# Parameter rows issued later, first gated products taken by token half, and three more convolution taps per tile moved into the mix turns

## The chip, the cores and the metric

The kernel runs on one core of one Trainium2 chip. The metric is the device time of one launch in microseconds (us). The core has TensorE (PE, matrix products; its weight loads are shown apart as PEld), VectorE (DVE), ScalarE (ACT), GpSimd (POOL) and SyncE (SP, which here only issues DMAs). Each engine works through its own queue in order and waits on semaphores that the others raise.

## What is computed

A block of a language model on 1024 tokens of width 1024, and behind it an attention block on the same tokens, in float32. Only the first part of the first block is touched:

```python
h = rmsnorm(x, g_mix[i])
z = jnp.einsum("bsd,dn->bsn", h, w_in[i])
a_val, a_gt = z[..., :o1], z[..., o1:o2]
sc_b, sc_c, sc_v = z[..., o2:o3], z[..., o3:o4], z[..., o4:o5]
gate_logits = z[..., o5:] + b_gate[i]
g_a = jax.nn.sigmoid(gate_logits[..., :D_MODEL])
g_b = jax.nn.sigmoid(gate_logits[..., D_MODEL:])
a = a_val * jax.nn.sigmoid(a_gt)
a = causal_dwconv(a, conv_a_w[i]) + conv_a_b[i]      # 31 taps, 512 channels
a = jax.nn.silu(layernorm(a, ln_a_g[i], ln_a_b[i]))
y_a = jnp.einsum("bsc,cd->bsd", a, w_a_out[i])
s = sc_b * causal_dwconv(sc_c * sc_v, conv_b_w[i])   # 3 taps
y_b = jnp.einsum("bsc,cd->bsd", s, w_b_out[i])
x = x + jnp.einsum("bsd,de->bse", g_a * y_a + g_b * y_b, w_o[i])
```

Behind it come a gated feed-forward part, a second gate, the attention block and the output; the change leaves them as they are, but for the count of a semaphore.

## The kernel before

All activations lie transposed: channels on the 128 partitions, the 1024 tokens along the row. Every matrix product is made of three products of split operands (high by high, low by high, high by low). A "slab" is 128 output channels of a weight: SP loads it into one of two `raw` buffers, POOL splits it into `whi` and `wlo` (L421, L422, L424), and PE takes it. A "job" is one such product, written to one of two pairs of PSUM banks (job number modulo 2): `gemm` (L482) waits until the pair is free and the slab is split, and issues for each of the 8 (or 4) blocks of input channels 6 matmuls of 512 tokens, so 48 (or 24) in all. DVE or ACT read the pair and raise `pair_free`. So PE can run at most about one pair of jobs ahead of DVE. POOL starts a slab's split when PE begins the slab before it.

The stages that the change touches, in order:

1. The x stage. Eight token tiles of x (128 tokens by 1024) are loaded by SP into two buffers `x_nat`; for each, ACT squares it and sums (L973), DVE scales the sum (L1286), ACT takes the root (L975), DVE the reciprocal (L1288) and the product `x_scaled` (L1292), PE transposes it in 8 blocks (L524), ACT copies it to `xa_hi` (L979) and DVE the remainder to `xa_lo` (L1296). Ahead of all this the queue of ACT issues the DMAs of the parameter rows (L953 to L967), 24 small loads into `rows`. Behind the eight tiles PE transposes the three blocks of `rows` (L552), DVE copies them to the table `tab` (L1299), ACT makes `silu_c` of it (L983), and only then PE begins the products.
2. The glu stage: four turns, each two jobs of 48 matmuls. ACT takes the sigmoid of the first (L988), DVE multiplies the second by it into `glu_pad` (L1342), and then does the first N1 = 14 of the 31 taps of the long convolution on that tile (`tap`, L1311 and L1315), each a scalar_tensor_tensor over 128x1024 that waits for the one before.
3. The short stage: four turns of three jobs. DVE does a 3-tap convolution (L1354 to L1362), N2 = 14 more taps of a tile of the long one, the product L1368, and the remainder `xb_lo` (L1373).
4. The mix stage: eight turns `mix_b`, then eight `mix_a`, each a gate job of 48 matmuls and a product job of 24. ACT takes the sigmoid of the gate (L1005), DVE the product (L1384 for mix_b). Behind the products of turns 0 and 1 DVE does the last N3 = 3 taps of two tiles each. Then it adds the four tiles (L1404, L1407) and takes the product of turn 2; PE sums over channels with a matrix of ones (L578) between turns 2 and 3; DVE subtracts the mean (L1411), ACT squares (L1012), PE takes column sums behind turn 3 (L531) and broadcasts the reciprocal root behind turn 4 (L541). ACT copies it to `rbc` (L1017), and in turn 5 DVE scales the four tiles (L1426), ACT makes the silu (L1022) and the high half (L1024), DVE the low half (L1430), tile by tile through one buffer. ACT takes the sigmoid of turn 5 only behind that. The first product job of mix_a needs the result.

Order on each queue is written out by hand; there is no planner.

Of the kernel before, what the change touches and what calls it, by code (L numbers as in the profile page):

```python
# [4 lines left out]
F32 = mybir.dt.float32  # L5
# [92 lines left out]
def build_program(nc, A, out, ydram):  # L98
# [41 lines left out]
    sqj = at("sq_junk", [P, D], F32, o_r + 5 * KB4)  # L140
# [105 lines left out]
    def settle(engine):  # L246


        engine.wait_ge(sem("consts_in"), 32)


    def sync_program(sp):
# [16 lines left out]
        sp.dma_start(xn[:, 0, :], A["x"][0, 0:P, :]).then_inc(sem("x_in0"), 16)  # L269
        sp.dma_start(gbc[:, :], A["g_mix"][0:1, :].to_broadcast([P, D])).then_inc(sem("g_in"), 16)  # L270
        sp.dma_start(xn[:, 1, :], A["x"][0, P:2 * P, :]).then_inc(sem("x_in1"), 16)
        slab8(L, w_in, DC, True)
        slab8(L + 1, w_in, 0, True)
        for t in range(2, 8):
            sp.wait_ge(sem("xs_ready"), t - 1)
            sp.dma_start(xn[:, t % 2, :], A["x"][0, t * P:(t + 1) * P, :]).then_inc(sem(f"x_in{t % 2}"), 16)
# [196 lines left out]
    def tensor_program(pe):  # L473
# [101 lines left out]
        mix_turns("mix_b", XBh[:, 4:8, :], XBl[:, 4:8, :], 1, 3)  # L575
# [4 lines left out]
        mix_turns("mix_b", XBh[:, 4:8, :], XBl[:, 4:8, :], 3, 4)  # L580
        column_sums(T[1], 8, 0, sem("ln_v"), 10)
        mix_turns("mix_b", XBh[:, 4:8, :], XBl[:, 4:8, :], 4, 5)
        broadcast(T[2][:, 0:1024].rearrange("p (t n) -> p t n", n=P), 8, 1)
        mix_turns("mix_b", XBh[:, 4:8, :], XBl[:, 4:8, :], 5, 8)
# [6 lines left out]
        for u in range(2):  # L591
            pe.wait_ge(sem(f"x_in{u}"), 8 * 16)
# [344 lines left out]
    def scalar_program(act):  # L937
# [8 lines left out]
        act.dma_start(rotm[:, :], A["rotate"]).then_inc(sem("consts_in"), 16)  # L946
        act.wait_ge(sem("consts_set"), 1)
# [22 lines left out]
        for t in range(9):  # L970
            if t < 8:
                act.wait_ge(sem(f"x_in{t % 2}"), 16 * (t // 2 + 1))
                fn(sqj[:, :], xn[:, t % 2, :], ACT.Square, accum_out=ssq[:, t:t + 1]).then_inc(sem("n1_sq"), 1)  # L973
                act.wait_ge(sem("row_var"), t + 1)
                fn(sd[:, t:t + 1], var[:, t:t + 1], ACT.Sqrt).then_inc(sem("row_sd"), 1)  # L975
            if t >= 1:
                J = Lin(JOBS["x"] + t - 1)
                act.wait_ge(job_done, J.val(1))
                fn(XAh[:, :, (t - 1) * P:t * P], pair(J).rearrange("p (m n) -> p m n", n=P), ACT.Copy).then_inc(sem("x_hi"), 1)  # L979

        act.wait_ge(sem("tab_ready"), 1)
        for k, name in enumerate(("c_2", "c_ctx_2")):
            fn(cs[:, :, k], tab[:, COL[name]:COL[name] + KD], ACT.Silu).then_inc(sem("cs"), 1)  # L983
        with act.Fori(0, KC) as i:
# [3 lines left out]
            fn(T[0][:, 0:S], pair(J), ACT.Sigmoid).then_inc(*one(free(J)))  # L988

# [17 lines left out]
        gate_sigmoid("mix_b", 0, 3, 8 + 5)  # L1007
        for i in range(4):
# [4 lines left out]
        gate_sigmoid("mix_b", 3, 4, 8 - 3)  # L1013
        root(8, 1)
        gate_sigmoid("mix_b", 4, 5, 8 - 3)
        act.wait_ge(sem("bc_pe"), 1)
        fn(rbc[:, :], PS[:, ST:ST + S], ACT.Copy).then_inc(sem("rbc_ready"), 1)  # L1017
        for i in range(4):
            act.wait_ge(sem("ln_n"), i + 1)
            if i >= 1:  # L1020
                act.wait_ge(sem("branch_lo"), 4 + i)
            fn(T[3][:, 0:S], T[1 + i % 2][:, 0:S], ACT.Silu, scale=col("ln_a_g", i), bias=col("ln_a_b", i)).then_inc(sem("a_silu"), 1)  # L1022
            act.wait_ge(sem("a_silu"), i + 1)
            fn(XBh[:, i, :], T[3][:, 0:S], ACT.Copy).then_inc(sem("branch_hi"), 1)  # L1024
        gate_sigmoid("mix_b", 5, 8, 8 - 3)
# [228 lines left out]
    def vector_program(dve):  # L1254
# [27 lines left out]
        dve.wait_ge(sem("g_in"), 16)  # L1282
        for t in range(9):
            if t < 8:
                dve.wait_ge(sem("n1_sq"), t + 1)
                ts(var[:, t:t + 1], ssq[:, t:t + 1], 1.0 / D, EPS, ALU.mult, ALU.add).then_inc(sem("row_var"), 1)  # L1286
                dve.wait_ge(sem("row_sd"), t + 1)
                nc.vector.reciprocal(rcp[:, t:t + 1], sd[:, t:t + 1]).then_inc(sem("row_rcp"), 1)  # L1288
# [3 lines left out]
                stt(xs[:, t % 2, :], xn[:, t % 2, :], rcp[:, t:t + 1], gbc[:, :], ALU.mult, ALU.mult).then_inc(sem("xs_ready"), 1)  # L1292
            if t >= 1:
                J = Lin(JOBS["x"] + t - 1)
                dve.wait_ge(sem("x_hi"), t)
                tt(XAl[:, :, (t - 1) * P:t * P], pair(J).rearrange("p (m n) -> p m n", n=P),  # L1296
                   f32(XAh[:, :, (t - 1) * P:t * P]), ALU.subtract).then_inc(*one(free(J)))
        dve.wait_ge(sem("tab_pe"), 1)
        nc.vector.tensor_copy(tab[:, :], PS[:, ST:ST + 3 * P]).then_inc(sem("tab_ready"), 1)  # L1299
# [578 lines left out]
```

## Time and profile before

| | us |
|---|---|
| median of three runs | 2226.7 |
| lowest and highest | 2226.05, 2227.9 |
| the profiled execution, as timed | 2228.41 |
| its span in the trace | 2226.6 |

| engine | busy us | share of span |
|---|---|---|
| PE | 2069.8 | 93% |
| PEld | 1711.0 | 77% |
| DVE | 1184.2 | 53% |
| ACT | 453.3 | 20% |
| POOL | 745.3 | 33% |

Times in the trace are counted from the start of the span. The page has a strip of each engine's busy share in 40 slices of 55.7 us; DVE stands at 4, 6, 8, 9, 9, 9, 5 in the first seven, and at 1 to 6 after. A busy PE is not a PE at its peak: its granted clock is a column of its own.

### The profile page before, as it was taken

To read this page: it belongs to the slowest core of one execution; us is meant where nothing else is said; L and a number is where in the kernel's file an instruction comes from. 1 tells how busy PE (TensorE), PEld (TensorE's weight loads), DVE (VectorE), ACT (ScalarE), POOL (GpSimd) and SP (SyncE) were. 2 spreads that over 40 slices of the span, in tenths; PEclk is the share of its full clock that TensorE was granted. 3 is DMA by queue.
4 is the path that set the end of the run, shared out by engine and by line. 5 is a ranking of instruction groups with operands and counts; after the bars stand their busy time and mean duration, and the time that the engine had idled before them with its cause. 6 is when DMAs were issued, how large, how long until landed. Compare 5 with 4: busy or idle time off the path is not lost.

```text
span 2226.6 us, 24771 instructions
## 1 busy us (share of the span) xinstructions
PE 2069.8 (93%) x9621; PEld 1711.0 (77%) x9621; DVE 1184.2 (53%) x1128; ACT 453.3 (20%) x558; POOL 745.3 (33%) x540
## 2 busy tenths in 40 slices
PE   4988999999998999999999999989689988999998
PEld 3876777788786788888888888768468867888877
DVE  4689995211543655655565655744441635556521
ACT  4100002200221100000000000233331125555511
POOL 1333454445332333333333333633132420212121
PEclk9999999999999999999999999999699998999999
DMA  4111111132113122112222112211131201000032
GB/s 127 47 38 38 43 39 42 42 92 74 57 38 114 48 66 67 47 52 71 75 66 66 47 47 75 76 29 38 29 112 31 90 15 25 10 11 1 1 123 85
DMA packets 176897, 122.04 MB, mean 55 GB/s; under 512 B 8820, under 2 KB 160321, under 8 KB 176833
## 3 DMA queue, kind: packets, MB, share of 16 engines
q1 hardware_dynamic: 175552, 118.77, 17.8%
q10 hardware_dynamic: 1280, 2.35, 0.3%
q8 instruction: 48, 0.79, 0.1%
q14 instruction: 17, 0.13, 0.0%
HBM read 112.71 MB, written 8.39 MB: 54 GB/s over the span
## 4 chain that ended last, share of the span: by engine, by line
PE 67%; DVE 17%; issue 4%; ACT 4%; POOL 4%; DMA 3%; DVEq 1%; ACTq 1%; SPq 0%; POOLq 0%
PE ps L482 55%; DVE conv_a L1315 8%; DMA raw<-in_w_up 2%; PE ps L764 2%; POOL wlo L424 1%; PE ps L531 1%; POOL rbc L443 1%; DVE prob L1694 1%; PE ps L541 1%; PE ps L797 1%; PE ps L799 1%; PE ps L778 1%; PE ps L798 1%; PE ps L775 1%; PE ps L781 1%
## 5 line engine op out<-in xcount | busy, mean ns | idle before, releaser
L424 POOL TENSOR_TENSOR wlo<-raw,whi 128x1024 fp32r<-128x1024 f32 (+2 forms) x162 | 455.4, 2811 | 13.5
L421 POOL TENSOR_TENSOR small<-ones 128x1 f32<-128x1 f32 x166 | 50.5, 304 | 1210.5 <-PE ps L482 1021.4
L482 PE MATMUL ps<-xb_hi,whi 128*128 128x512 f32 x1216 | 384.3, 398 | 42.4 <-DVE xb_lo L1593 16.4
L482 PE MATMUL ps<-xa_hi,whi 128*128 128x512 f32 x1184 | 374.9, 398 | 34.8 <-DVE t L1369 8.1
L482 PE MATMUL ps<-xb_lo,whi 128*128 128x512 f32 x1216 | 379.9, 394 | 0.0
L482 PE MATMUL ps<-xb_hi,wlo 128*128 128x512 f32 x1216 | 379.6, 394 | 0.0
L482 PE MATMUL ps<-xa_lo,whi 128*128 128x512 f32 x1184 | 368.7, 393 | 0.0
L482 PE MATMUL ps<-xa_hi,wlo 128*128 128x512 f32 x1184 | 368.3, 392 | 0.0
L482 PEld LDWEIGHTS ps<-xb_hi,whi 128*128 128x128 f32 x1216 | 228.9, 191 | 102.3 <-DVE xb_lo L1593 15.9
L482 PEld LDWEIGHTS ps<-xa_hi,whi 128*128 128x128 f32 x1184 | 223.7, 191 | 85.9 <-issue 34.2
L482 PEld LDWEIGHTS ps<-xb_lo,whi 128*128 128x128 f32 x1216 | 231.8, 191 | 49.5
L482 PEld LDWEIGHTS ps<-xb_hi,wlo 128*128 128x128 f32 x1216 | 231.6, 190 | 49.2
L482 PEld LDWEIGHTS ps<-xa_lo,whi 128*128 128x128 f32 x1184 | 225.4, 190 | 47.9
L482 PEld LDWEIGHTS ps<-xa_hi,wlo 128*128 128x128 f32 x1184 | 224.6, 190 | 47.6
L1315 DVE SCALAR_TENSOR_TENSOR conv_a<-glu_pad,tab,conv_a x120 | 199.5, 1662 | 20.7 <-DVE conv_a L1315 19.9
L422 POOL TENSOR_SCALAR whi<-raw 128x1024 fp32r<-128x1024 f32 (+2 forms) x162 | 174.1, 1075 | 0.2 <-issue 0.2
L1063 ACT ACTIVATE t<-t 128x1024 f32<-128x1024 f32 x22 | 23.3, 1061 | 515.2 <-DVE t L1486 515.2
L461 POOL TENSOR_SCALAR prob<-prob,small 128x1280 f32<-128x1280 f32 x32 | 43.0, 1343 | 229.5 <-DVE small L1703 229.5
L1499 DVE TENSOR_TENSOR resid<-ps,resid 128x1024 f32<-128x1024 f32 x80 | 97.8, 1222 | 35.0 <-PE ps L482 33.8
L1481 DVE TENSOR_TENSOR t<-ps,rbc 128x1024 f32<-128x1024 f32 x22 | 26.9, 1224 | 135.0 <-PE ps L482 130.2
L1486 DVE SCALAR_TENSOR_TENSOR t<-t,tab,t 128x1024 f32<-128x1024 f32 x44 | 93.4, 2122 | 6.2 <-DVE t L1483 1.4
L1686 DVE TENSOR_TENSOR pt_lo<-ps,pt_hi 128x512 fp32r<-128x512 f32 (+1 forms) x96 | 56.3, 598 | 40.7 <-ACT pt_hi L1179 40.6
(320 smaller groups left out, 2275.5 us busy)
## 6 DMA issues: line engine op xcount, KB each, us to landing
raw<-in_w_in SPq DMA_DIRECT2D x52, 512.0 KB, 3.8
raw<-in_w_up SPq DMA_DIRECT2D x44, 512.0 KB, 4.0
raw<-in_w_down SPq DMA_DIRECT2D x22, 512.0 KB, 3.6
w_mod<-in_w_mod SPq DMA_DIRECT2D x40, 256.0 KB, 2.8
x_nat<-in_x SPq DMA_DIRECT2D x8, 512.0 KB, 3.6
x_columns<-in_x SPq DMA_DIRECT2D x8, 512.0 KB, 5.1
raw<-in_w_o SPq DMA_DIRECT2D x8, 512.0 KB, 3.8
raw<-in_w_ple_gate SPq DMA_DIRECT2D x8, 512.0 KB, 3.8
```

The lines of the kernel that those rows point to most:

```text
L421: nc.gpsimd.tensor_tensor(small[:, 30 + slab.slot:31 + slab.slot], ones[:, 0:1], ones[:, 0:1], ALU.mult)
L422: nc.gpsimd.tensor_scalar(hi, src, 1.0, 0.0, ALU.mult, ALU.add).then_inc(sem("split_hi"), 1)
L424: nc.gpsimd.tensor_tensor(lo, src, f32(hi), ALU.subtract).then_inc(split_done, 1)
L461: nc.gpsimd.tensor_scalar(Pr[t % 2][:, :], Pr[t % 2][:, :], rsum4[:, t % 4:t % 4 + 1], 0.0, ALU.mult, ALU.add).then_inc(sem("p_scaled"), 1)
L482: ins = mm(dst[j], w, r[j], start=first and f, stop=last and l)
L764: last = nc.tensor.transpose(PS[:, o:o + P], Pr[a][:, k * P:(k + 1) * P], ident[:, :])
L1063: fn(T[2][:, 0:S], T[1][:, 0:S], ACT.Gelu_apprx_tanh).then_inc(sem("gelu"), 1)
L1315: stt(tile(conv, i), tile(gpad, i, k, k + S), dcol("conv_a_w", i + 4 * k), tile(conv, i), ALU.mult, ALU.add).then_inc(sem("conv_tap"), 1)
L1481: tt(T[0][:, 2:2 + S], pair(Jg), rbc[:, :], ALU.mult).then_inc(*one(free(Jg)))
L1486: stt(T[1][:, 0:S], T[0][:, w:w + S], dcol("conv_f_w", n + (k + NF * w)), T[1][:, 0:S], ALU.mult, ALU.add).then_inc(sem("fc_tap"), 1)
L1499: tt(R[:, m, :], pair(J + m), R[:, m, :], ALU.add).then_inc(*one(free(J + m)))
L1686: tt(PTl[:, k0:k1, cols], PS[:, o:o + (k1 - k0) * P].rearrange("p (t n) -> p t n", n=P), f32(PTh[:, k0:k1, cols]), ALU.subtract).then_inc( ...
```

## The change

What it does, part by part:

- SP: x is loaded into eight tiles of `x_nat` (now in the space of `xb_hi`); tiles 0 and 1 one by one, the first slab, tiles 2 and 3 in one DMA, tiles 4 and 5 (behind the first `x_scaled`), the second slab, tiles 6 and 7 (behind the second).
- ACT: a Sqrt on a constant stands ahead of the x stage. The parameter rows are issued behind the eight tiles. The square of tile t+2 and the root of tile t+1 stand ahead of the copy of tile t.
- The transposes of x write to the other half of PSUM. PE does the tiles 0 to 4, then the first glu job on tokens 0 to 511 in pieces between the transposes of tiles 5, 6 and 7, then the second job on these tokens, then both on tokens 512 to 1023; then the rows are transposed. `silu_c` no longer stands ahead of the products.
- N1 is 12, N2 13, N3 6. The last taps, 24 in all, are done 8 each behind the products of mix_b turns 0, 1 and 2; the adds come behind the product of turn 3.
- The sum with ones stands behind turn 4, the column sums behind turn 5, the broadcast behind turn 6, and the normalisation, silu and split in turn 7, in place in `conv_a`, with ACT no longer waiting for the low half of the tile before.

The core of the diff:

```diff
-    xn = at("x_nat", [P, 2, D], F32, o_r)
+    xn = at("x_nat", [P, 8, D], F32, o_xbh)
...
+        x_rows(0, 1, "x_in0")
+        sp.dma_start(gbc[:, :], A["g_mix"][0:1, :].to_broadcast([P, D])).then_inc(sem("consts_in"), 16)
+        x_rows(1, 1, "x_in1")
         slab8(L, w_in, DC, True)
+        x_rows(2, 2, "xn_in2")
+        sp.wait_ge(sem("xs_ready"), 1)
+        x_rows(4, 2, "x_in0")
         slab8(L + 1, w_in, 0, True)
...
+        pe.wait_ge(sem("consts_in"), 48)
+        for t in range(5):
+            x_transposes(t)
+        pe.wait_ge(split_done, 1)
+        pe.wait_ge(pair_free[0], 2)
+        pe.wait_ge(pair_free[1], 2)
+        glu_half(0, 0, range(0, 3))
+        x_transposes(5)
+        glu_half(0, 0, range(3, 7))
+        x_transposes(6)
+        glu_half(0, 0, range(7, 8))
+        pe.wait_ge(split_done, 2)
+        glu_half(1, 0, range(0, 3))
+        x_transposes(7)
+        glu_half(1, 0, range(3, 8))
+        pe.wait_ge(pair_free[0], 4)
+        pe.wait_ge(pair_free[1], 4)
+        glu_half(0, 1, range(KD))
+        glu_half(1, 1, range(KD))
         pe.wait_ge(sem("rows_in"), N_ROW_DMAS * 16)
...
-        pe.wait_ge(sem("cs"), 2)
-        pe.wait_ge(pair_free[0], 4)
-        pe.wait_ge(pair_free[1], 4)
-        with pe.Fori(0, KC) as i:
+        with pe.Fori(1, KC) as i:
...
-        mix_turns("mix_b", XBh[:, 4:8, :], XBl[:, 4:8, :], 1, 3)
+        mix_turns("mix_b", XBh[:, 4:8, :], XBl[:, 4:8, :], 1, 5)
         pe.wait_ge(sem("ln_v"), 3)
...
+        act.wait_ge(sem("consts_set"), 2)
+        fn(sd[:, 12:13], ones[:, 0:1], ACT.Sqrt)
...
+        x_square(0)
+        x_root(0)
+        x_square(1)
+        for t in range(8):
+            if t < 6:
+                x_square(t + 2)
+            if t < 7:
+                x_root(t + 1)
+            J = Lin(JOBS["x"] + t)
+            act.wait_ge(job_done, J.val(1))
+            fn(XAh[:, :, t * P:(t + 1) * P], x_pair(J).rearrange("p (m n) -> p m n", n=P), ACT.Copy).then_inc(sem("x_hi"), 1)
...
-        N1 = 14
+        N1 = 12
...
+        glu_product(0)
+        dve.wait_ge(sem("tab_pe"), 1)
+        nc.vector.tensor_copy(tab[:, :], PS[:, ST:ST + 3 * P]).then_inc(sem("tab_ready"), 1)
...
-        N3 = 3
+        N3 = 6
...
+        for m in range(3):
+            mix("mix_b", m, m + 1, False)
+            last_taps(8 * m, 8 * m + 8)
+        mix("mix_b", 3, 4, False)
...
-        for i in range(5):
+        for i in range(6):
             if i < 4:
-                if i >= 2:
-                    dve.wait_ge(sem("a_silu"), i - 1)
-                tt(T[1 + i % 2][:, 0:S], conv[:, i, :], rbc[:, :], ALU.mult).then_inc(sem("ln_n"), 1)
-            if i >= 1:
-                dve.wait_ge(sem("branch_hi"), 4 + i)
-                dve.wait_ge(sem("ln_n"), i)
-                tt(XBl[:, i - 1, :], T[3][:, 0:S], f32(XBh[:, i - 1, :]), ALU.subtract).then_inc(sem("branch_lo"), 1)
-        mix("mix_b", 5, 8, False)
+                tt(conv[:, i, :], conv[:, i, :], rbc[:, :], ALU.mult).then_inc(sem("ln_n"), 1)
+            if i >= 2:
+                dve.wait_ge(sem("branch_hi"), 3 + i)
+                tt(XBl[:, i - 2, :], conv[:, i - 2, :], f32(XBh[:, i - 2, :]), ALU.subtract).then_inc(sem("branch_lo"), 1)
+        mix("mix_b", 7, 8, False)
```

## Rows read from the trace of the kernel before

**Rows 1.** The page: the chain that ended last, by engine, then by line.
```profile
PE 67%; DVE 17%; issue 4%; ACT 4%; POOL 4%; DMA 3%; DVEq 1%; ACTq 1%; SPq 0%; POOLq 0%
```

**Rows 2.** Windows: stretch, length, busy (instructions) of PE, PEld, DVE, ACT, POOL, clock, DMA.
```profile
70.70:443.70 373.00, 343.67 (x1466) 278.96 (x1466) 282.78 (x184) 46.06 (x42) 152.74 (x102) 0.96 0.14 40
152.00:160.00 8.00, 5.93 (x14) 4.68 (x15) 7.23 (x5) 1.03 (x1) 4.41 (x3) 0.58 0.01 2
1573.00:1604.00 31.00, 17.45 (x46) 11.08 (x46) 12.23 (x21) 10.06 (x11) 2.10 (x3) 0.50 0.00 0
```

**Rows 3.** Waits of PE, 71 to 444 us: us in total, times, longest.
```profile
PE ps L482 <- DVE t L1369: 8.1, 3, 6.3
PE ps L482 <- DVE glu_pad L1342: 6.9, 2, 4.3
PE ps L482 <- ACT t L1005: 5.2, 1, 5.2
PE ps L578 <- DVE t L1407: 3.9, 1, 3.9
PE ps L482 <- DVE xb_lo L1373: 3.7, 1, 3.7
PE ps L482 <- DVE t L1354: 1.5, 1, 1.5
```

**Rows 4.** Timeline of the start: start us, us, engine, line; idle before.
```profile
11.39 0.33 ACTq L967 DMA_DIRECT2D rows<-in_c_ctx  x1
13.04 1.06 ACT L973 ACTIVATE sq_junk<-x_nat 128x1024 f32<-128x1024 f32 x1
17.69 1.94 PE L524 MATMUL ps<-ident,x_scaled 128*128 128x128 f32 x8 [17.69 <-DVE x_scaled L1292]
41.33 1.97 PE L524 MATMUL ps<-ident,x_scaled 128*128 128x128 f32 x8 [1.68 <-DVE x_scaled L1292]
46.75 1.21 PE L482 MATMUL ps<-xa_hi,whi 128*128 128x512 f32 x2 [2.81 <-ACT silu_c L983]
49.47 1.05 PE L482 MATMUL ps<-xa_hi,whi 128*128 128x512 f32 x2
51.48 0.62 PE L482 MATMUL ps<-xa_hi,whi 128*128 128x512 f32 x2
70.85 1.23 DVE L1342 TENSOR_TENSOR glu_pad<-ps,t 128x1024 f32 x1 [24.60 <-PE ps L482]
```

**Rows 5.** DMA issues in narrow windows of the start: count, KB each, median us to landing.
```profile
x_nat<-in_x SPq DMA_DIRECT2D x1, 512.0 KB, 4.1
raw<-in_w_in SPq DMA_DIRECT2D x2, 512.0 KB, 9.8
```

**Rows 6.** Groups of DVE, 71 to 347.3 us: busy us, mean ns, idle before.
```profile
L1315 DVE SCALAR_TENSOR_TENSOR conv_a<-glu_pad,tab,conv_a x120 | 199.5, 1662 | 20.7 <-DVE conv_a L1315 19.9 <-DVE conv_a L1311 0.7
```

**Rows 7.** Splits (L424) in the same stretch: length, POOL busy (count), clock, DMA.
```profile
71.00:347.30 276.30, 76.05 (x24) 0.97 0.14 42
```

**Rows 8.** Timeline of DVE around one split, four taps.
```profile
81.75 1.29 DVE L1315 SCALAR_TENSOR_TENSOR conv_a<-glu_pad,tab,conv_a  x1 [0.18 <-DVE conv_a L1315]
83.22 1.96 DVE L1315 SCALAR_TENSOR_TENSOR conv_a<-glu_pad,tab,conv_a  x1 [0.18 <-DVE conv_a L1315]
85.36 3.15 DVE L1315 SCALAR_TENSOR_TENSOR conv_a<-glu_pad,tab,conv_a  x1 [0.18 <-DVE conv_a L1315]
```

**Rows 9.** Timeline of the norm's steps, 347 to 408 us.
```profile
347.45 3.48 PE L578 MATMUL ps<-t,ones 128*128 128x512 f32 x4 [3.86 <-DVE t L1407]
385.47 1.88 PE L541 MATMUL ps<-t,ones 128*128 128x512 f32 x4
388.44 4.90 DVE L1426 TENSOR_TENSOR t<-conv_a,rbc 128x1024 f32<-128x1024 f32 x2 [1.56 <-ACT rbc L1017]
406.38 1.28 ACT L1005 ACT_TABLE_LOAD   x1
407.67 1.11 ACT L1005 ACTIVATE t<-ps,tab 128x1024 f32<-128x1024 f32 x1
```

More of the change, by code:

```diff
@@ L220, in pair, with x_pair @@
         return PS[0:p, 1024 * job.slot + a:1024 * job.slot + b]
+    def x_pair(job):
+        return PS[:, ST + 1024 * job.slot:ST + 1024 * (job.slot + 1)]
     def f32(ap):
@@ L542, in broadcast, with x_transposes, glu_half @@
             last.then_inc(sem("bc_pe"), 1)
-        pe.wait_ge(sem("consts_in"), 32)
-        for t in range(8):
+        def x_transposes(t):
             pe.wait_ge(sem("xs_ready"), t + 1)
-            transposes(Lin(JOBS["x"] + t), [xs[:, t % 2, k * P:(k + 1) * P] for k in range(KD)])
+            if t >= 2:
+                pe.wait_ge(pair_free[t % 2], t // 2)
+            for k in range(KD):
+                last = nc.tensor.transpose(x_pair(Lin(t))[:, k * P:(k + 1) * P], xs[:, t % 2, k * P:(k + 1) * P], ident[:, :])
+            last.then_inc(job_done, 1)
+        def glu_half(u, c, ks):
+            J, L = Lin(JOBS["glu"] + u), Lin(SLABS["glu"] + u)
+            q = slice(H * c, H * (c + 1))
+            for k in ks:
+                last = split_products([pair(J, H * c, H * (c + 1))], whi[:, L.slot, k * P:(k + 1) * P], wlo[:, L.slot, k * P:(k + 1) * P],
+                                      [XAh[:, k, q]], [XAl[:, k, q]], k == 0, k == KD - 1, 1 if c and k == 0 else None)
+            if c:
+                last.then_inc(job_done, 1)
+        pe.wait_ge(sem("consts_in"), 48)
[17 more added lines that the diff above has]
+        glu_half(1, 1, range(KD))
         pe.wait_ge(sem("rows_in"), N_ROW_DMAS * 16)
@@ L968, in scalar_program, with glu_sigmoid @@
                 r += n
[L970 to L984, printed above, removed]
+        def glu_sigmoid(i):
             J = Lin(JOBS["glu"], 2, i)
@@ L988, in scalar_program @@
             fn(T[0][:, 0:S], pair(J), ACT.Sigmoid).then_inc(*one(free(J)))
+        glu_sigmoid(0)
+        act.wait_ge(sem("tab_ready"), 1)
+        for k, name in enumerate(("c_2", "c_ctx_2")):
+            fn(cs[:, :, k], tab[:, COL[name]:COL[name] + KD], ACT.Silu).then_inc(sem("cs"), 1)
+        with act.Fori(1, KC) as i:
+            glu_sigmoid(i)
         act.wait_ge(*free(Lin(JOBS["short"] - 1)))
@@ L1335, in mod_mac, with glu_product @@
                 stt(acc, w, cs[:, k, n:n + 1], acc, ALU.mult, ALU.add).then_inc(sem("mod_mac"), 1)
-        N1 = 14
-        with dve.Fori(0, KC) as i:
+        N1 = 12
+        def glu_product(i):
             J = Lin(JOBS["glu"], 2, i)
@@ L1343, in vector_program @@
             dve.wait_ge(*free(J + 1))
+        glu_product(0)
+        dve.wait_ge(sem("tab_pe"), 1)
+        nc.vector.tensor_copy(tab[:, :], PS[:, ST:ST + 3 * P]).then_inc(sem("tab_ready"), 1)
+        dve.wait_ge(sem("tab_ready"), 1)
+        for k in range(N1):
+            tap(0, k, k)
+        with dve.Fori(1, KC) as i:
+            glu_product(i)
             for k in range(N1):
                 tap(i, k, i * N1 + k)
-        N3 = 3
+        N3 = 6
         N2 = TAPS_A - N1 - N3
@@ L1376, in vector_program, with last_taps, mix @@
                     tap(i, k, i * N2 + (KC * N1 + k - N1))
-        def mix(name, a, b, add, taps=False):
+        def last_taps(a, b):
+            for n in range(a, b):
+                i, k = n // N3, n % N3
+                tap(i, N1 + N2 + k, KC * (N1 + N2) + n)
+        def mix(name, a, b, add):
             with dve.Fori(a, b) as m:
@@ L1384, in mix @@
                     tt(tile(R, m + (5 if a < 3 else -3)), pair(J + 1), T[0][:, 0:S], ALU.mult).then_inc(*one(free(J + 1)))
-                    for v in range(2 if taps else 0):
-                        i = m * 2 + v
-                        for k in range(N1 + N2, TAPS_A):
-                            tap(i, k, i * N3 + (KC * (N1 + N2) + k - N1 - N2))
                 else:
```

77 lines of the change are left out of this document (43 added, 34 removed).

## The prediction

> **What bounds the kernel now.** I read the page first. PE is busy 93% of the span, yet the chain that ended last goes by DVE for 17% of it [rows 1]: there is a stage in which DVE sets the pace. The strip of the page puts it in the first seven slices. The windows then give its size. Call G the moment at which DVE can take the first gated product (70.85 us, the last of rows 4). PE's first product of mix_a begins at 443.7. Between 70.7 and 443.7 PE is busy 343.7 of 373.0 us [rows 2], and it waits 29.3 us in all, in every row for DVE or for something that stood behind DVE [rows 3]. The reader should see in these rows that no wait is for a DMA or a split.
>
> How much of that PE needs at full clock: 1440 matmuls (3 glu pairs of 96, 12 short jobs of 48, 8 mix turns of 72). Two take 0.62 us and overlap by a third [rows 4]; 48 of them run in 10.9 us, which is 0.227 each, so 326.9 us. The column sums 1.7, the broadcast 1.88 less overlap, 1.7, and the sum with ones, which ran at the low clock for 3.48, 1.75 at the high one [rows 9]: 332.1 in all. Busy less needed is 11.6 us: that is the clock. A stretch with a 4.3 us wait in it was granted 0.58 of the full 2.4 GHz [rows 2]. So between G and mix_a up to 40.9 us are to be had, 29.3 of waits and 11.6 of clock.
>
> Ahead of G lie 70.85 us. ACT issues parameter rows until 11.7 and squares its first tile at 13.04 [rows 4], though the tile was issued at 0.74 and landed 4.1 later [rows 5]. The transposes start at 17.69 and come 3.38 apart, (41.33 - 17.69)/7; the first product waits 5.4 us more, for the table and silu_c; the first matmuls run at the low clock (two in 1.05 instead of 0.62) [rows 4]. Behind 443.7 PE's order and its waits are as before, relative to one another, so what is gained up to there is kept.
>
> **Part 1, the start: G.** ACT begins tile 0 at 4.9. From the first square to the first transposes took 4.65 with a table load of 1.28 inside; that load is now done before, so the transposes of tile 0 start at 8.3. Tile 1 then waits: ACT has the square of tile 2 ahead of the root of tile 1, and tiles 2 and 3 come behind the first slab. The two slabs of before landed 9.8 us after their issue at 2.1 to 3.0, with five loads of 512 KB in flight [rows 5]; six are now ahead, less the rows' small packets. I take 13.5. Square, root, reciprocal and product (1.25, 0.2, 0.2, 1.3, and hops) put the transposes of tile 1 at 16.6. From there a tile costs DVE 1.28 + 1.22 + two small ones, and the loop product, root, reciprocal, product about 3.2 with its hops, little less than the 3.38 of before. Tiles 2, 3, 4 transpose at 19.6, 22.8, 26.0, PE is free at 28.0.
>
> From here PE does not stop. Tokens 0 to 511 are there when tile 3's remainder is, 27.3. Nine cold matmuls (0.427 each) end at 31.8; tile 5, 33.6; twelve at full clock 36.4; tile 6 and three, 38.1; nine, 40.2; tile 7, 41.3; fifteen, 44.7. Tile 7's remainder is ready near 43.6, so no wait. Then 48 matmuls, 10.9: G is at 55.6. That is 15.2 earlier than 70.85, of which some 8 from the rows and 7 from products that fill PE between transposes and stand ahead of the table. Bounds: 53 if the loads land at 11, 60 if the tiles keep 3.38 apart and the clock rises only behind tile 7.
>
> The moved rows must not become the wait. ACT issues them behind tile 7's copy, at 42.4; they took 9.9 us of its queue and nearly 3 more to land, so 55.3 against 55.6: cover gone to within 0.3 us. Queued behind them on ACT is the first sigmoid (1.28 load and 1.03), ready at 54.7. Each microsecond of lateness costs one, as DVE needs the table for tap 0. I take 0 and keep 3 for the range. The table's transposes and copy, now behind G, cost 0.6.
>
> **Part 2, from G to the adds: DVE's sum.** From the first product to the end of the adds (347.3) DVE took 276.5 us and never starved; of this 124 taps, the rest small. A tap alone is 1.28, the mean over 120 is 1.66 [rows 6], because each split of POOL stretches two of them, 0.68 and 1.87 [rows 8]. There were 24 splits [rows 7]; over all DVE lines the stretch is 57.9 us, 2.4 a split. The taps themselves are only moved, 56, 56, 12 to 48, 52, 24: they cost what they did. New ahead of the adds' end are two products (turns 2 and 3, 1.2 each), the table 0.6 and its hop, and the splits of slabs that PE now begins in that time, 28 for 24, 9.6: 276.5 + 2.4 + 0.7 + 9.6 = 289.2, and one split less if the last falls behind the adds; I take 288.
>
> Is that DVE's time still or PE's? A glu turn costs DVE 1.5 + 1.0 + 11 x 1.465 + 4.8 = 23.5 (26.4 before) against 21.8 of PE; a short turn 33.0 (34.5) against 32.7; a mix turn 17.7 against 16.35. So DVE is late by 2 us a turn in glu, 7 at its end, within the 9.7 that PE can run ahead; one wait of 4 us comes in the first short turn (6.35 before); then both go level to the end, PE at 286.6 and DVE at 286.9 from G by the turns. The two sums differ by 1 to 2 us. Where more goes wrong on PE, it and not DVE is late there, which is the upper bound, 293; where splits stretch less, 285.
>
> The Trainium skill, SBUF — State Buffer, section "Who interferes with whom", says that a DVE instruction with two SBUF inputs and a GpSimd one that reads SBUF lock each other out for the whole instruction. Taken in full, a split would cost DVE up to 3.4 and not 2.4, and the four more splits 4 us more; the rows show two taps stretched, not one blocked for 3.4.
>
> **Part 3, the norm.** Behind the adds: ones 1.75, turn 5 16.35, column sums 1.7, turn 6 16.35, broadcast 1.7, turn 7 16.35: 54.2. Before, two waits lay in it, 3.9 at the ones and 5.2 at the sigmoid behind the normalisation [rows 3]. The first goes: the product of turn 3 stands ahead of the adds and frees PE's pair, so PE does the product job of turn 4 meanwhile (5.45 for 5.8 of adds). For the second: in turn 7 the scaling starts 1.1 behind the turn, its first two tiles took 4.9 with a split in them [rows 9]; four silu and copies of 2.3 each go back to back on ACT since each tile has its own place; table load 1.28, sigmoid 1.1 done at 15.3 of 16.35. Cost 0, at most 1. The low halves end 15 us before mix_a's first product job asks for them.
>
> The Trainium skill, ScalarE: Activation LUTs, section "What ACT_TABLE_LOAD costs", adds about 1.4 us of drain to each load. By it the sigmoid would be 2 us late. The rows show the load at 406.38 for 1.28 and the sigmoid at 407.67, so none [rows 9].
>
> **The sum.** 55.6 + 288 + 54.2 = 397.8, against 443.7: 45.9 us less. The profiled span 2226.6 becomes 2180.7; 1.8 lies around it, and the profiled run stands 1.7 above the median: 2226.7 - 45.9 = 2180.8, and a low clock at the ones, as there was before (3.48 instead of 1.75 [rows 9]), is as likely as not: half of 1.7 more. I say 2182.
>
> **The rivals.** (a) The start gives less: the loads of x or the order of ACT hold tiles back, or the rows come late. G is 60 to 64: 2187 to 2192. For it: the square of tile 2 ahead of tile 1's root, and 0.3 us of cover. (b) PE becomes the bound in the short and mix stages: a longer wait brings a low clock with it (0.58 over 8 us around a wait of 4.3 [rows 2], so 8 x 0.42 = 3.4 us of it, less what falls into the wait), 2 to 3.4 us each; three such beyond the forecast, 2188 to 2194. Against it: lags shrink everywhere. (c) DVE meets fewer splits or G is earlier: 2170 to 2176; PE's own sum, 55.6 + 0.5 + 332.1, allows 2171. (d) Slower than before: the clock. If PE, with pieces of products between transposes, were granted 1.2 GHz through the conv stages, each microsecond at it loses half. It decides from 92 us of low clock more (45.9 x 2). The longest such stretch here is near 31 us, with PE waiting half of it [rows 2]; unlikely. (e) The change doesn't do what it says: the early products wait for the remainder of tile 7 and DVE's pace is unchanged, because the stage is bound by its 124 taps, of which none is removed. Then only the 8 us of the rows and 12 taps' worth of work moved behind count: no less than 8, no more than 20, 2207 to 2219.
>
> **How the numbers follow.** Forecast, 2176 to 2187: 0.60. (a) 0.14, (b) 0.10, (c) 0.10, (d) 0.02, (e) 0.02; no change for a reason not seen 0.02. The range takes in the forecast, most of (a), (b) and (c): 2174 to 2193. What a measurement of this kernel can tell from no change is about 0.2%, 4.5 us. Faster 0.96, same 0.02, slower 0.02.
>
> **What would show it.** The first transposes near 8.3, the last near 40, G between 54 and 58. In the stretch from G to mix_a PE waits 5 to 12 us, not 29, and the clock is 0.98 or more. A mean tap stays at 1.65. The glu waits of PE are gone; one for the short product stays. L578 comes 288 after G. If the product of turn 7 follows its sigmoid with a wait of PE, part 3 was wrong; if PE waits for rows, the cover was; if anything behind mix_a differs by over 1 us, the claim that the gain is kept falls.

## The result, and the profile after

| | before | after |
|---|---|---|
| median of four runs, us | 2226.38 | 2172.06 |
| lowest and highest | 2222.58, 2227.9 | 2168.68, 2176.38 |
| the profiled execution, as timed | 2228.41 | 2176.38 |
| its span | 2226.6 | 2174.6 |

The ratio is 0.9757, with a 95% interval of 0.9744 to 0.9771: 54 us less, where 45 were forecast, and 2 us below the low end of the range. The profiled execution of after is the slowest of its four, 4.3 us above the median, so the two traces are 52.0 us apart and not 54.

The stages as the prediction cut them, in the two profiled executions (G is DVE's first gated product; "ones" is the start of the sum with ones):

| | before | forecast | after |
|---|---|---|---|
| start to G | 70.85 | 55.6 | 53.8 |
| G to ones | 276.6 | 288 | 283.8 |
| ones to mix_a's first product | 96.3 | 54.2 | 55.1 |
| start to mix_a | 443.7 | 397.8 | 392.7 |
| mix_a to the end | 1782.8 | 1782.8 | 1781.9 |

Of the 52.0 us between the two spans 51.0 lie ahead of mix_a; the stretch behind it is 0.9 shorter, and among all the kernels here that stretch differs by up to 6 us (below).

The page of after has the line that answers [rows 1]; lines of the code stand nine to some eighty further down than before (L482 is now L491, the taps L1383, the gated product L1411).

```profile
PE 70%; DVE 14%; POOL 5%; issue 4%; ACT 3%; DMA 3%; DVEq 1%; SPq 0%; POOLq 0%; ACTq 0%
```

The windows of after, from G to ones, from ones to mix_a, and behind mix_a. Columns: stretch, length, busy time and (instructions) of PE, PEld, DVE, ACT, POOL, granted clock, DMA share, GB/s.

```profile
53.83:337.60 283.77, 280.48 (x1226) 230.52 (x1225) 260.55 (x164) 20.74 (x21) 133.87 (x84) 0.99 0.16 46
337.60:392.70 55.10, 54.98 (x243) 44.10 (x242) 26.72 (x22) 22.88 (x21) 24.73 (x18) 1.00 0.15 43
392.70:2174.50 1781.80, 1681.86 (x7994) 1395.55 (x7992) 873.02 (x904) 381.39 (x477) 585.99 (x425) 0.97 0.19 56
```

In the first 338.9 us behind G PE is busy 335.5, at 0.99 of the full clock; before it was busy 343.7 of 373.0 at 0.96 [rows 2]. What is left of its waits, in the place of the six rows of [rows 3] (us in total, times, longest):

```profile
PE ps L491 <- DVE xb_lo L1451: 2.0, 1, 2.0
PE ps L491 <- POOL wlo L433: 1.3, 3, 0.5
```

29.3 us of waits became 3.3, and 1.3 of that is for splits and not for DVE at all. Behind the one wait for DVE the matmuls follow one another by 0.43 us instead of 0.227, eight in a row, at a granted clock of 0.57 from 262.9 to 266.8, which adds 1.7 us. The same wait in `rows_first` (below) is 1.92 us long, and the clock stays at 1.00 behind it:

```profile
262.86 1.11 PE L491 MATMUL ps<-xb_hi,whi 128*128 128x512 f32 x2 [1.96 <-DVE xb_lo L1451]
265.73 0.73 PE L491 MATMUL ps<-xb_hi,whi 128*128 128x512 f32 x2 [1.92 <-DVE xb_lo L1451]
```

The timeline of DVE at the end of its taps shows the order of things turned round (start us, us, engine, line; in brackets the idle time before and who ended it):

```profile
311.61 16.02 DVE L1383 SCALAR_TENSOR_TENSOR conv_a<-glu_pad,tab,conv_a 128x1024 f32<-128x1024 f32 x8
330.00 2.56 DVE L1491 TENSOR_TENSOR t<-t,conv_a 128x1024 f32<-128x1024 f32 x2
337.82 1.22 DVE L1468 TENSOR_TENSOR resid<-ps,t 128x1024 f32<-128x1024 f32 x1 [5.27 <-PE ps L491]
```

The adds end at 332.56, 278.7 behind G, and then DVE waits 5.27 us for PE. Before, PE waited 3.9 us at this place for DVE [rows 3]. DVE no longer sets the pace; PE does.

### The profile page after: what moved, and what is told of

Read it like the earlier page. It is cut to its first block, busy times and chain, and to the rows that moved or that the text cites. A ratio compares the mean times of both kernels' runs of the same rounds, so it can differ in the third digit from the quotient of the medians.

```text
span 2174.6 us, 24666 instructions
## 1 busy us (share of the span) xinstructions
PE 2053.6 (94%) x9621; PEld 1700.2 (78%) x9621; DVE 1183.6 (54%) x1128; ACT 447.7 (21%) x556; POOL 756.5 (35%) x540
## 4 chain that ended last, share of the span: by engine, by line
PE 70%; DVE 14%; POOL 5%; issue 4%; ACT 3%; DMA 3%; DVEq 1%; SPq 0%; POOLq 0%; ACTq 0%
PE ps L491 58%; DVE conv_a L1383 5%; DMA raw<-in_w_up 2%; POOL wlo L433 2%; PE ps L803 2%; POOL whi L431 1%; POOL rbc L452 1%; PE ps L540 1%; DVE prob L1776 1%; PE ps L550 1%; PE ps L836 1%; PE ps L817 1%; PE ps L814 1%; PE ps L820 1%; PE ps L811 1%
## 5 line engine op out<-in xcount | busy, mean ns | idle before, releaser
L433 POOL TENSOR_TENSOR wlo<-raw,whi 128x1024 fp32r<-128x1024 f32 (+2 forms) x162 | 459.4, 2836 | 13.5
L491 PE MATMUL ps<-xb_hi,whi 128*128 128x512 f32 x1216 | 384.2, 398 | 42.0 <-DVE xb_lo L1675 18.4
L491 PE MATMUL ps<-xa_hi,whi 128*128 128x512 f32 x1184 | 374.0, 395 | 12.9 <-DVE xa_lo L1516 5.1
L491 PE MATMUL ps<-xb_lo,whi 128*128 128x512 f32 x1216 | 380.1, 394 | 0.0
L491 PE MATMUL ps<-xb_hi,wlo 128*128 128x512 f32 x1216 | 379.5, 394 | 0.0
L491 PE MATMUL ps<-xa_lo,whi 128*128 128x512 f32 x1184 | 369.5, 391 | 0.0
L491 PE MATMUL ps<-xa_hi,wlo 128*128 128x512 f32 x1184 | 369.2, 391 | 0.0
L491 PEld LDWEIGHTS ps<-xb_hi,whi 128*128 128x128 f32 x1216 | 229.1, 191 | 101.4 <-DVE xb_lo L1675 17.3
L491 PEld LDWEIGHTS ps<-xb_lo,whi 128*128 128x128 f32 x1216 | 231.8, 191 | 49.5
L491 PEld LDWEIGHTS ps<-xb_hi,wlo 128*128 128x128 f32 x1216 | 231.6, 190 | 49.4
L491 PEld LDWEIGHTS ps<-xa_hi,whi 128*128 128x128 f32 x1184 | 221.7, 189 | 62.0 <-issue 6.5
L491 PEld LDWEIGHTS ps<-xa_hi,wlo 128*128 128x128 f32 x1184 | 223.5, 189 | 47.1
L491 PEld LDWEIGHTS ps<-xa_lo,whi 128*128 128x128 f32 x1184 | 223.7, 189 | 46.9
L1383 DVE SCALAR_TENSOR_TENSOR conv_a<-glu_pad,tab,conv_a (+1 forms) x120 | 205.9, 1716 | 14.3 <-DVE conv_a L1383 12.6
```

What stands on the lines that cost most here:

```text
L433: nc.gpsimd.tensor_tensor(lo, src, f32(hi), ALU.subtract).then_inc(split_done, 1)
L491: ins = mm(dst[j], w, r[j], start=first and f, stop=last and l)
L1383: stt(tile(conv, i), tile(gpad, i, k, k + S), dcol("conv_a_w", i + 4 * k), tile(conv, i), ALU.mult, ALU.add).then_inc(sem("conv_tap"), 1)
```

## The experiments

Ten kernels besides the two. The first four, the next four and the last two were each run on one chip, with runs of before beside them (medians 2227.05, 2227.17 and 2227.21). Where a row is compared between kernels it is from one profiled execution of each.

### The two halves of the change apart

`start_only` is the changed kernel with the taps and the norm of before; `mix_only` is before with the taps and the norm of after.

```diff
# start_only, against after (the mix turns and norm of DVE, ACT and PE as before)
-        N1 = 12
+        N1 = 14
...
-        N3 = 6
+        N3 = 3
# mix_only, against before (the mix turns and norm of DVE, ACT and PE as after)
-        N1 = 14
+        N1 = 12
...
-        N3 = 3
+        N3 = 6
```

> The changed start (loads, order of ACT, products by token half, rows behind the x stage) with the taps 14, 14, 3 and the norm where they were. My theory: the start is worth G (first gated product taken by DVE) 70.85 to 53.8, so 17 us, and DVE still sets the pace behind it, its sum from G to the adds near 276 less 1.6 for the first glu turn, whose taps are now written out one by one; 2226.4 becomes about 2208. Rival: the start's gain is partly eaten because PE waits longer for DVE later: over 2213. Rival: the start is worth more than its 17 us: under 2204.

Measured: 2206.9 (ratio 0.9909, 0.9893 to 0.9926), G at 53.4, ones 273.0 behind it, mix_a 96.4 behind that. The start is worth 20 us: in the traces 17.5 at G, and 3.5 more in DVE's sum behind it, where 1.6 were expected for the unrolled turn.

> The start of before, with taps 12, 13, 6 and the norm in turn 7. Theory: from G to mix_a's first product 373 becomes about 339 to 341, so about 2226.4 - 33 = 2193, and this and the start add up to the whole 54. Rival (what I had forecast): DVE's sum sets it, 288 to the adds and 342 to mix_a, 2196. Rival: the two parts need one another (without the early start DVE falls behind at the beginning): over 2200.

Measured: 2194.6 (0.9854, 0.9838 to 0.9871): G at 70.5, and then 338.0 us to mix_a, where after takes 338.9. So 32 us for this half and 20 for the other: together 52 to 53 of 54. They add up, within the 3 to 4 us of the intervals; no sign that either needs the other or takes from it. The windows from G to ones, start_only first, then mix_only (its ones to mix_a takes 55.1 as in after):

```profile
53.30:326.40 273.10, 253.75 (x1084) 207.39 (x1082) 251.64 (x163) 18.61 (x19) 117.88 (x72) 0.96 0.15 44
70.50:353.40 282.90, 278.46 (x1224) 229.07 (x1223) 260.14 (x163) 20.42 (x19) 135.50 (x84) 1.00 0.15 45
```

In mix_only DVE is busy 260 of 283 us and PE 278: with the taps spread over three more mix turns both are nearly full, and the clock stays at its upper level (1.00) throughout, also behind its longest wait of 2.1 us.

### Is PE the bound behind G?

`fewer_taps` leaves out the last 24 taps, so the convolution has 25 of its 31 taps.

```diff
         for m in range(3):
             mix("mix_b", m, m + 1, False)
-            last_taps(8 * m, 8 * m + 8)
...
-        dve.wait_ge(sem("conv_tap"), KC * (N1 + N2) + 2 * N3)
+        dve.wait_ge(sem("conv_tap"), KC * (N1 + N2))
```

> The changed kernel without its last 24 taps (the convolution has 25 of 31 taps; that part of the computation is left out). Theory: PE is now the bound from G to mix_a, the adds end 5 us before PE asks for them, so 24 taps less (some 41 us of DVE) give nothing but the three waits of 0.45 us for splits: 2170 to 2172. Rival: DVE still sets the pace: 2172 - 30 or more, under 2150.

Measured: 2173.3 (0.9753, 0.9737 to 0.9769), the same as after within both intervals, 1.3 above the range that was expected. DVE is busy 216 instead of 261 us of the stretch, and the stretch is 2.3 us shorter:

```profile
54.00:335.50 281.50, 279.53 (x1227) 230.73 (x1225) 216.07 (x140) 20.73 (x21) 126.30 (x84) 0.99 0.16 47
```

So 44 us of DVE work are worth at most 2.3 us: PE is the bound in the mix turns. Taking the taps away removes its three waits for splits (1.3 us): the split just ahead of the first of these waits took POOL 2.04 and 3.23 us in after, 1.05 and 2.40 here. The kernel keeps the wait of 2.0 for DVE and the low clock behind it, as both come before the taps that it leaves out. For the glu and short turns it shows nothing, but there the rows of after do: PE is busy all of the 146.2 us from 53.8 to 200, and that wait is the only one up to the first mix turn. It and the clock behind it are 3.7 us in which DVE still counts.

### Why DVE's sum was 9 us too high

The forecast had 288 us from G to the end of the adds; it took 278.7. I compared the steps of the taps. Written out one by one they show as a single group of one shape in the timeline, looped ones as single lines without a shape. Undisturbed, the former follow one another by 1.32 us, the latter by 1.466, as the gap of 0.18 in [rows 8] against 0.04. `static_before` writes out DVE's loops of before and changes nothing else:

```diff
         N1 = 14
-        with dve.Fori(0, KC) as i:
+        for i in range(KC):
...
         N3 = 3
         N2 = TAPS_A - N1 - N3
-        with dve.Fori(0, 2) as q:
+        for q in range(2):
# and the two mix turns that hold taps likewise
```

> Before, with nothing changed but that DVE's glu turns, short turns and the two mix turns with taps are written out instead of looped, so that addresses and counts are constants. Theory: a tap follows the one before by 1.32 instead of 1.466 us, 0.145 less on each of 116 dependent taps and on some others, so DVE's sum from G to the adds is 17 to 19 us shorter and the time 2226.4 - 17 = 2209 (a few us less of that if PE becomes the later one). Rival: the shorter step in the changed kernel came from the place in the program and not from the constants: no change, 2226.

Measured: 2213.1 (0.9932, 0.9915 to 0.9948), 14 us less than before. G to ones went from 276.6 to 261.9. Four undisturbed taps from the start of the first to the end of the last, which in a loop would be 3 x 1.466 + 1.285 = 5.68:

```profile
77.68 5.25 DVE L1315 SCALAR_TENSOR_TENSOR conv_a<-glu_pad,tab,conv_a 128x1024 f32<-128x1024 f32 x4
```

The undisturbed step is (5.25 - 1.285) / 3 = 1.32. Some 2 to 3 us of the expected 17 are not there. The rows show where they went. There are 24 splits in either kernel, and the excess of DVE's lines over undisturbed operations, their stretch by the splits, is 61.9 us here and 58.0 in before. The three taps around the first split take 6.75 us from the start of the first to the end of the third:

```profile
82.96 6.75 DVE L1315 SCALAR_TENSOR_TENSOR conv_a<-glu_pad,tab,conv_a 128x1024 f32<-128x1024 f32 x3
```

In before they take as much, from 83.22 to 89.97, though each starts 0.18 behind the one before. The middle one is stretched to 3.30 here and to 3.15 there, and in both it ends 1.08 us after POOL's second operation: a tap that is held by a split ends with the split, and starting sooner gains it nothing. DVE also waits 1.1 us for PE here.

Which part of a looped tap costs it? A tap waits for the one before by a count and has its addresses computed. `tap_forms` meant to take one from a register and the other as a constant, in loops of one turn:

```diff
         def last_taps(a, b):
-            for n in range(a, b):
-                i, k = n // N3, n % N3
-                tap(i, N1 + N2 + k, KC * (N1 + N2) + n)
+            for i in range(KC):
+                ns = [n for n in range(a, b) if n // N3 == i]
+                if ns:
+                    with dve.Fori(i, i + 1) as r:
...
+                            at, base = r if a != 8 else i, KC * (N1 + N2) + n
+                            dve.wait_ge(sem("conv_tap"), base if a == 0 else r + (base - i))
```

> The changed kernel with the last taps in three forms: in mix turn 0 the addresses come from a register and the counts waited for are constants, in turn 1 the addresses are constants and the counts come from a register, in turn 2 both come from a register. Theory: the 0.145 us between 1.32 and 1.466 come from one of the two. If from the addresses, undisturbed taps follow one another by 1.466 in turns 0 and 2 and 1.32 in turn 1; if from the counts, 1.32 in turn 0 and 1.466 in 1 and 2; a third theory is that both cost half. The time moves by no more than 1 us, as DVE has 5 us to spare there.

Measured: 2173.1 in one run, and all three turns stepped by 1.32 us. It tells nothing: the rows show a constant shape (the first of the three below), so a loop of one turn was made into constants, and the three forms were one.

```profile
277.53 16.01 DVE L1466 SCALAR_TENSOR_TENSOR conv_a<-glu_pad,tab,conv_a 128x1024 f32<-128x1024 f32 x8
```

The same eight took 16.02 in after. `probe` uses true loops of two turns, with spare operations in DVE's idle time behind mix_b:

```diff
         mix("mix_b", 7, 8, False)
+        with dve.Fori(0, 2) as r:
+            for n in range(3):
+                probe(r + n, r + n, spare[n], tile(R, r + n), r * 3 if n == 0 else None)
+        for n in range(3):
+            probe(n, n, spare[n], tile(R, n), 6 if n == 0 else None)
+        with dve.Fori(0, 2) as r:
+            for n in range(3):
+                probe(n, n, spare[0], spare[0], r * 3 + (9 + n))
+        for n in range(3):
+            probe(n, n, spare[0], spare[0], 15 + n)
```

> The changed kernel with 18 spare scalar_tensor_tensor operations of a tap's shape on DVE between mix_b and mix_a, results unused: six in a loop of two turns with addresses from a register and no wait between the three of a turn; three with constant addresses and no wait; six in a loop of two turns with constant addresses, each waiting for the one before by a count from a register; three with constants, each waiting by a constant count. Theory: the 0.145 us that a looped tap takes more is the register: it shows where the wait's count is from a register (steps of 1.46 there, 1.32 in the last three) and not where only addresses are. Rival: it shows in the first group, by the addresses (against steps of 1.2 to 1.3 in the second). Rival: in both, half each. The time is 15 to 20 us longer, as mix_a's first product waits for DVE.

Measured: 2180.2 in one run, 8 us above after; 15 to 20 were expected, and that part of the expectation missed. Addresses from a register and no wait: a step of 1.20, as with constants and no wait. Constant addresses and a count from a register: 1.32 in the undisturbed turn, as with constants throughout. Only where an operation has both a wait and register addresses (the first of the loop's second turn, the one such place in this kernel that follows another spare operation) is the gap 0.18 us. In these rows the operation at 397.19 follows a wait, the two at 398.39 do not:

```profile
395.74 1.27 DVE L1518 SCALAR_TENSOR_TENSOR t<-resid,tab 128x1024 f32 x1
397.19 1.28 DVE L1518 SCALAR_TENSOR_TENSOR rbc<-resid,tab 128x1024 f32 x1 [0.18 <-DVE t L1518]
398.39 2.47 DVE L1518 SCALAR_TENSOR_TENSOR t<-resid,tab 128x1024 f32 x2
```

The view of the taps' line says what fills the gap: register operations of DVE's own queue (DVEq), 93 ns each. First before, then after (count; duration in ns, min/median/max; first and last start):

```profile
L1315 DVEq FUSED_REGOPS  x128: 76/93/99, 75.3 to 339.4; - x128
L1383 DVEq FUSED_REGOPS  x89: 82/93/104, 80.4 to 273.1; - x89
```

The first of before starts at 75.3, when the operation before ends (72.39 + 2.89 = 75.28), and the tap starts at 75.47: the addresses are computed behind the wait, and so stand in the open. Without a wait they are computed while the operation before runs (in `probe` the last register operation of the loop starts at 397.6, inside the operation of 397.19 to 398.47). Neither theory was right: it takes the wait and the register addresses together. After has 35 constant taps (11 of the first glu turn, 24 of the mix turns) where the forecast priced all at 1.466: 35 x 0.145 = 5.1 us, with what splits take back of it counted in their stretch.

### What the start is made of

`rows_first` puts the parameter rows ahead of the x stage again; `whole_tokens` does all eight transposes first and the products behind them.

```diff
# rows_first: the block of ACT's row DMAs moved up
         act.dma_start(rotm[:, :], A["rotate"]).then_inc(sem("consts_in"), 16)
+        act.wait_ge(sem("consts_set"), 1)
+        for b, bin_ in enumerate(ROWS):
...
         act.wait_ge(sem("consts_set"), 2)
         fn(sd[:, 12:13], ones[:, 0:1], ACT.Sqrt)
# whole_tokens, on PE
-        for t in range(5):
+        for t in range(8):
             x_transposes(t)
...
+        for u in range(2):
+            pe.wait_ge(split_done, u + 1)
+            for c in range(2):
+                glu_half(u, c, range(KD))
```

> The changed kernel with the parameter rows issued by ACT ahead of the x stage again. ACT then begins tile 0 at 13.1 instead of 5.2, but tile 1, which waited for the load of tiles 2 and 3 until 15.66, comes near 19: G 3 to 4 us later, the time 2172.5 + 3.5 = 2176. Rival (my forecast's split of the start's gain): 8 us later, 2180. Rival: the rows were never in the way because the loads set the pace, 0 to 1.

Measured: 2177.2 (0.9776, 0.9761 to 0.9791), G at 56.7, 2.9 later than after. The expectation nearly held at G (3 to 4) and in the time, and the forecast's 8 us did not. But the 5 us by which the medians differ are not in the traces: at ones they are only 0.6 apart (338.2 against 337.6), as this kernel has one split wait less (0.4) and no low clock behind the wait for DVE (1.7). What the rows are worth is so not settled between 0.6 in the traces and 5 in the medians.

> The changed kernel with PE doing all eight tiles' transposes first and the two glu jobs behind them. Theory: the pieces between the transposes fill PE and also bring it to the full clock before the bulk of the products; without them PE starts the products near 39.5 with nine or ten matmuls at the low clock: G near 63, 9 to 10 us later, 2182. Rival (forecast's split): 7 us, of which 1.5 clock, 2179.

Measured: 2185.6 (0.9814, 0.9799 to 0.9829), G at 62.4, 8.5 later, where 9 to 10 were expected. At ones the traces are 6.3 apart (343.9 against 337.6), since after has one split wait more (0.4) and the low clock behind its wait for DVE (1.7), which is 1.9 us long and followed by the full clock here. The medians are 13.5 apart, some 7 more than that: 4.3 because the profiled execution of after is that much above its median, 1.5 because the one of whole_tokens is below its own, and 1.4 behind mix_a, where the profiled executions of all these kernels differ by up to 6 us without order (1778.6 to 1784.6).

So of 17.0 us at G, 2.9 are lost if the rows come back alone, 8.5 if the pieces go alone. Both shares together are 11.4. The other 5.6 may be the order of ACT, the loads into eight tiles and the table off PE's path, or what the rows and the pieces hide of each other; no run takes this apart.

### Two attempts to better the start

In after, the transposes of tile 1 wait 5.23 us, since ACT has the square of tile 2, and its load, ahead of the root of tile 1:

```profile
12.85 1.06 ACT L992 ACTIVATE sq_junk<-x_nat 128x1024 f32<-128x1024 f32 x1 [3.18 <-DMA x_nat<-in_x]
15.66 1.97 PE L560 MATMUL ps<-ident,x_scaled 128*128 128x128 f32 x8 [5.23 <-DVE x_scaled L1359]
```

```diff
# root_first
-            if t < 6:
+            if 1 <= t < 6:
                 x_square(t + 2)
...
+            if t == 0:
+                x_square(2)
# loads_first: root_first, and on SP
-        slab8(L, w_in, DC, True)
         x_rows(2, 2, "xn_in2")
+        slab8(L, w_in, DC, True)
```

> The changed kernel with ACT's square of tile 2 moved behind the root of tile 1 and the copy of tile 0, so that ACT does not stand at the load of tiles 2 and 3. Theory: the transposes of tile 1 go from 15.66 to near 12, those of tile 2 from 18.25 to 16 to 17, G 1 to 3 us earlier: 2170. Rival: the next load (tiles 4 and 5, issued behind the first x_scaled) or DVE's split contention at tile 3 takes it back: 0.

Measured: 2171.9 (0.9747, 0.9734 to 0.9760). In the trace tile 1 starts at 11.48, G is at 51.0 and mix_a at 389.8, each 2.8 earlier than in after. As timed it can't be told from after: the expected 2170 is within its interval, but so is no gain.

> The kernel with the square of tile 2 moved, and in it the load of tiles 2 and 3 ahead of the first weight slab. Theory: tile 2 lands near 11 instead of 12.85, its transposes start near 14.5 instead of 16.6, and G is another 1.5 to 2.5 us earlier than its 51.0, mix_a's first product near 388: some 5 us less than the changed kernel in the trace and 2167 to 2170 as timed. Rival: the slab's split now falls onto DVE's steps of tiles 2 to 4 and takes it back: G 51.

Measured: 2171.6 (0.9753, 0.9740 to 0.9767), G at 52.4, so 1.3 later than root_first: at G the rival held. The square of tile 2 starts at 11.38 instead of 12.68, but then its product meets the split of the first slab and takes 3.43 us instead of 1.28; that of tile 3 takes 3.27:

```profile
13.95 3.43 DVE L1361 SCALAR_TENSOR_TENSOR x_scaled<-x_nat,small,g_mix_bc 128x1024 f32<-128x1024 f32 x1
13.96 2.34 POOL L433 TENSOR_TENSOR wlo<-raw,whi 128x1024 fp32r<-128x1024 f32 x1
```

Yet loads_first starts mix_a at 389.0, 0.9 ahead of root_first (389.9) and 3.7 ahead of after (392.7), as the clock stays at 1.00 behind its wait for DVE (1.9 us) and it has a split wait less: with the later G it lost 1.3 and got back 2.2. As timed, no version beats after clearly; both are ahead of it in the traces up to mix_a alone.

## Why the prediction was wrong, point by point

- **The direction and the mechanism were right.** DVE set the pace from G to the norm and the start had an idle PE; both went as forecast, the waits at the ones and at the sigmoid are gone, and what was gained ahead of mix_a was kept. The size was 45 of 54.
- **Where the 9.9 us between 2182 and 2172.06 lie.** In the spans 6.1 (2180.7 forecast, 2174.6 measured): 1.8 at G, 4.2 from G to ones, 0.9 lost again in the norm, 0.9 behind mix_a. Then 1.2 that were added for a low clock at the ones and for rounding. The last 2.6 are no step of the kernel: the profiled execution was taken to stand 1.7 above the median, as before, and stood 4.3 above it. Had the median stood 1.7 below that execution, it would have been 2174.7, inside the range; that it lies outside is in part chance.
- **Part 1, G: 53.8 for 55.6.** The tiles' times were met closely (8.49 for 8.3, 15.66 for 16.6, 25.40 for 26.0). The first piece of products started at 27.25, not 28.0, and the clock rose at its end: the transposes of tile 5 took 1.03 us, where I had used 1.8 (start us, us):

```profile
29.95 0.63 PE L491 MATMUL ps<-xa_hi,whi 128*128 128x512 f32 x1
31.09 1.03 PE L560 MATMUL ps<-ident,x_scaled 128*128 128x128 f32 x8
```

  The split of the gain was wrong: "some 8 from the rows and 7 from products" was measured as 2.9 and 8.5, each undone alone. The times of the tiles had it that with the rows gone ACT stands at the load of tiles 2 and 3 (tile 1 at 16.6); the split of the gain had not, and so most of the rows' 8 us come back as a wait of 5.23.
- **The rows' cover.** It was put at 0.3 us. PE did not wait: G and the table follow the products without a gap. ACT issued the first row at 39.43, 3 us before the 42.4 of the forecast, in part because its queue went on to the rows while the copy of tile 7 (39.42 to 40.45) still ran.
- **Part 2 is the step that failed: "The taps themselves are only moved, 56, 56, 12 to 48, 52, 24: they cost what they did."** The 35 that were also written out cost 0.145 less each, 5.1 us. The stretch by splits was sized a little high as well: 57.9 and 9.6 are 67.5, some 66 with the 1.2 that were taken off for a split, against 63.6 over 27 splits (51.7 on the taps, as 205.9 less 120 x 1.285, 6.6 on the first taps, 3.1 and 2.2 on two other lines). 5.1 and 2.5 make 7.6 of the 9.3 by which 288 was above 278.7; the rest is unassigned.
- **DVE's time or PE's?** The forecast set both level, 286.6 and 286.9 from G, with DVE the later. With DVE at 278.7 to the adds' end PE was the later and set 283.8, so that only 4 of the 9 us counted. Its one wait of 4 us in the first short turn did not come, since DVE was ahead by then; a wait of 2.0 at the first mix turn came instead. `fewer_taps` shows that DVE's taps in the mix turns no longer count.
- **Part 3, the norm: 55.1 for 54.2.** No wait in it: PE is busy 54.98 of 55.1, so the 0.9 are in the sum of PE's own work. The sum with ones took 1.88 at the full clock (it had 3.48 [rows 9]), and the low clock that I had called as likely as not did not come. The sigmoid of turn 7 ran at 389.89 to 391.01, 1.7 before PE asked; the forecast had 1.05. That and the load just ahead of it are the row for the table load:

```profile
388.60 1.28 ACT L1064 ACT_TABLE_LOAD   x1
389.89 1.12 ACT L1064 ACTIVATE t<-ps,tab 128x1024 f32<-128x1024 f32 x1
```

- **The signs.** PE's waits from G to mix_a were put at 5 to 12 us and came to 3.3; one for the short product was to stay and none did. The mean tap was to stay at 1.65 and was 1.72 (205.9 over 120): 27 splits in place of 24 fall on the same number of operations, which that sign had left out though the sum had it.
- **The rule of the ScalarE page** (the Trainium skill, ScalarE: Activation LUTs, "What ACT_TABLE_LOAD costs", 1.4 us of drain) found no support again: 0.01 us lies between the two rows above, and 0.02 between the copy before (387.51 to 388.58) and the load.
- **The rule of the SBUF page** (the Trainium skill, SBUF — State Buffer, "Who interferes with whom") would have made four more splits dearer by 4 us; the stretch was 2.36 us a split over 27 splits, not more than before. What the rule says in kind is seen: in `loads_first` a product of DVE took 2.15 us longer than alone beside a POOL operation of 2.34 that began with it, and the tap held by the first split ends 1.08 us after POOL's operation in before and in `static_before` alike. What failed is the reading of it as 3.4 us a split.
- **The rivals.** The time is that of (c), which had 0.10: "PE's own sum, 55.6 + 0.5 + 332.1, allows 2171". Of its reasons G was earlier (1.8) and one split was not met; the taps written out are not among them. It deserved more. My own turn-by-turn account had PE and DVE within 0.3 us of each other, so an error of either sign in DVE's sum could only be cut off on one side, by PE. The range's low end at 2174 was above PE's sum of 2171, although nothing in the trace excluded reaching it.

## What to carry to other kernels

When two engines are level in the forecast, take the bound of the engine that isn't counted as late (here PE's own work, 332 us) as the near end of the range, for that is where the time goes if the other's sum is too high. When work is moved, ask also whether its form changes: from a loop to written-out code, a chain of dependent operations loses its address arithmetic, 0.145 of 1.466 us each here unless a split holds it, and `static_before` got 14 us from that alone. An edit that removes a delay ahead of a queue in order is worth only the time to the next wait in that queue: 8 us of DMA issues were worth 2.9 at G, and at ones 0.6 of them were left.

## What the runs showed of the hardware that was not expected

- On DVE, an operation in a loop that has to wait for the one before starts 0.18 us after it, against 0.04 for one with constant addresses; 93 ns of this is a register operation, which begins only when the wait is over. Register addresses without a wait, and a wait by a register count with constant addresses, cost nothing (1.20 and 1.32 us a step, as with constants).
- A tap that meets a split gains nothing from constant addresses: three taps around a split took 6.75 us looped and written out, and the held one ended 1.08 us after POOL's operation in both.
- Loops of a single turn showed as constants: the steps were 1.32 us.
- Splitting a slab took POOL's second operation 3.2 to 3.3 us beside taps and 2.34 to 2.4 alone; three times in after this made PE wait, 0.4 to 0.5 us each.
- The length of a wait near 2 us did not decide the clock behind it. In every kernel with the taps 12, 13, 6 PE waits for the last `xb_lo`: after 1.96, root_first 1.96, tap_forms 1.95 and fewer_taps 1.97 us had a granted clock of 0.55 to 0.60 behind it, rows_first, whole_tokens, loads_first and probe with 1.91 to 1.92 and mix_only with 2.07 had 1.00. It is 1.7 us of difference between kernels that do the same work there.
- Pieces of products between transposes kept PE going from 25.4 us on, and from about 31 its matmuls ran at the upper level (0.227 us from one to the next instead of 0.43); in before, where transposes came with 1.3 to 1.7 us between them, matmuls still ran at the lower level (two in 1.05 us) at 49.5 [rows 4]. The column of the granted clock does not show this: it reads 1.00 from 24 to 31 us in after and from 47 to 51 in before. In whole_tokens, with gaps of 0.6 to 1.2 us between the last transposes, the first eight matmuls of the products ran at the lower level too.
